# Gathering expert rows in two rounded passes, with the router worked by token tile and expert places released earlier

## The reference

```python
g_prob = softmax((xt @ w_rg) + b_rg)                  # 4 groups
g_w, g_idx = top_k(g_prob, 1)
e_logits = ((xt @ w_re) + b_re).reshape(t, 4, 8)      # 8 experts in each group
e_top, e_loc = top_k(e_logits of the chosen group, 2)
e_w = softmax(e_top) * g_w
# each token goes through its two experts:
y = (silu(xb @ w_gate[e]) * (xb @ w_up[e])) @ w_down[e]
out = sum over both of e_w * y
x = x + gate2 * out ; x = rms_norm(x, g_final)
```

## Time and profile before

| | us |
|---|---|
| runs shown | 1332.38, 1331.24, 1333.41 (median 1332.38) |
| the profiled execution | 1332.06 |
| span of the profile (first to last instruction) | 1329.5 |
| TensorE busy | 1306.5 (98%) |
| VectorE busy | 792.0 (60%) |
| ScalarE busy | 566.5 (43%) |
| mean transfer rate | 280 GB/s |

### The profile page before, as it was taken

How to read it: one execution, slowest core, us unless ns; L and a number is a source line. 1 busy time by engine, 2 the same in 40 slices (tenths; PEclk the granted TensorE clock), 3 DMA queues, 4 the chain that set the end, 5 groups by cost and what they waited for, 6 DMA issues and landing times.

```text
span 1329.5 us, 19339 instructions
## 1 busy us (share of the span) xinstructions
PE 1306.5 (98%) x7854; PEld 969.7 (73%) x7854; DVE 792.0 (60%) x1397; ACT 566.5 (43%) x859; POOL 33.7 (3%) x55
## 2 busy tenths in 40 slices
PE   8999999999999999999999999999999999999997
PEld 8988789999887997999987888754444544444442
DVE  5755598888986655898896877743222322223223
ACT  5344545655546576655645746531111111111122
POOL 0200010000001000100010000000000000000000
PEclk9999999999999999999999999999999999999999
DMA  9467286767585732555665563599999999999995
GB/s 355 162 223 260 100 303 226 237 210 252 202 289 174 241 140 96 183 188 178 252 226 190 209 250 127 197 400 409 428 428 426 429 429 427 429 427 427 428 422 206
DMA packets 113373, 371.83 MB, mean 280 GB/s; under 512 B 4604, under 2 KB 64284, under 8 KB 100368
## 3 DMA queue, kind: packets, MB, share of 16 engines
q1 hardware_dynamic: 105648, 344.07, 67.2%
q0 software_dynamic: 7648, 26.72, 5.7%
HBM read 369.71 MB, written 1.05 MB: 279 GB/s over the span
## 4 chain that ended last, share of the span: by engine, by line
PE 86%; DMA 7%; DVE 4%; ACT 2%; SPq 1%; issue 1%; DVEq 0%; ACTq 0%
PE ps L675 15%; PE ps L1590 14%; PE ps L635 9%; PE ps L636 9%; PE ps L637 9%; PE ps L1613 7%; PE ps L1572 4%; PE ps L652 4%; PE ps L654 3%; PE ps L653 3%; DMA arena<-in_w_expert_gate_dram 3%; DMA arena<-in_w_expert_down_dram 3%; PE ps L1619 2%; DVE w_low L570 1%; DMA const<-in_const_dram 1%; PE ps L1264 1%
## 5 line engine op out<-in xcount | busy, mean ns | idle before, releaser
L570 DVE TENSOR_TENSOR w_low<-ring,w_high 128x1024 fp32r<-128x1024 f32 x264 | 311.4, 1221 | 96.9 <-ACT w_high L562 96.1
L562 ACT ACTIVATE w_high<-ring 128x1024 fp32r<-128x1024 f32 x264 | 264.6, 1050 | 177.0 <-PE ps L675 82.9
L635 PE MATMUL ps<-h_high,w_high 128*128 128x256 f32 x1088 | 310.5, 285 | 0.8 <-DVE h_low L479 0.6
L636 PE MATMUL ps<-h_low,w_high 128*128 128x256 f32 x1088 | 307.8, 283 | 0.0
L637 PE MATMUL ps<-h_high,w_low 128*128 128x256 f32 x1088 | 307.7, 283 | 0.0
L635 PEld LDWEIGHTS ps<-h_high,w_high 128*128 128x128 f32 x1088 | 208.6, 192 | 6.4 <-issue 4.4
L636 PEld LDWEIGHTS ps<-h_low,w_high 128*128 128x128 f32 x1088 | 208.7, 192 | 0.0
L637 PEld LDWEIGHTS ps<-h_high,w_low 128*128 128x128 f32 x1088 | 208.6, 192 | 0.0
L1590 PE MATMUL ps<-ring,arena 128*64 128x512 f32 x592 | 176.6, 594 | 3.0 <-DMA arena<-in_w_expert_gate_dram 1.3
L1590 PEld LDWEIGHTS ps<-ring,arena 128*64 128x64 f32 x592 | 56.3, 137 | 111.8 <-issue 111.7
L675 PE MATMUL ps<-w_high,h_high 128*128 128x512 f32 x304 | 95.0, 394 | 1.0 <-DVE arena L2379 0.9
(11 more groups left out here) (402 smaller groups left out, 1679.8 us busy)
## 6 DMA issues: line engine op xcount, KB each, us to landing
ring<-in_ffn_w_up_dram SPq DMA_DIRECT2D x44, 1024.0 KB, 7.7
ring<-in_w_expert_gate_dram SPq DMA_DIRECT2D x19, 2048.0 KB, 25.0
ring<-in_w_expert_up_dram SPq DMA_DIRECT2D x18, 2048.0 KB, 21.5
ring<-in_w_expert_down_dram SPq DMA_DIRECT2D x17, 2048.0 KB, 26.2
ring<-in_ret_w_in_dram SPq DMA_DIRECT2D x11, 2048.0 KB, 8.0
arena<-in_w_expert_up_dram SPq DMA_DIRECT2D x11, 2048.0 KB, 27.7
ring<-in_ffn_w_down_dram SPq DMA_DIRECT2D x10, 2048.0 KB, 8.3
arena<-in_w_expert_gate_dram SPq DMA_DIRECT2D x9, 2048.0 KB, 23.1
```

Source lines behind the costliest of these rows:

```text
L562: nc.scalar.activation(hi, raw, ACT.Copy).then_inc(hi_done, 1)
L570: last = eng.tensor_tensor(lo, raw, hi.bitcast(F32), ALU.subtract)
L635: nc.tensor.matmul(o, hi, hTh[:, k, :], start=(k == 0 if whole else n == 0), stop=False, skip_group_check=not whole)
L636: nc.tensor.matmul(o, hi, hTl[:, k, :], start=False, stop=False, skip_group_check=not whole)
```

## The change

- `gather` becomes two rounded passes. ScalarE writes the normed rows rounded (`xn_hi`, in the place of `xn`), VectorE writes what is left (`rows_low`: x times the root, less the high part) into `xn_lo`. The low part of tile 1 lies over `rowv` and that of tile 0 over a stretch before it; `sel` becomes fp32r. Per feature block and token tile there are now two matmuls, high and low, each with a stationary tile of its own: 32 rounded matmuls in a gather in place of 16 four-byte ones.
- The first gather (pair 0) is written out by token tile: high of tile 0, high of tile 1, then low of both.
- The router is worked tile by tile on VectorE: `logits`, `group`, `experts`, `position`, `first_select` for tile 0, then for tile 1. Squares and roots go by tile. Casts of the indices fall away (the comparison is made with the integer index); iota counts from 1.
- `idle_turns` in the router go. The starting sums of tile 1 and the matmuls for the largest count move into the middle of gate of pair 0 (`start_second`).
- Places: home 6 waits for `l_t` 2 and not for `b_oc` 4, which takes an attention buffer (`mb_pT`) out of its way; the order of homes changes; half of the tile in home 1 is loaded after the third split of mix_out; one of the homes 4 and 5 (`EARLIER`) is loaded one half of mix_out earlier. Home 9 now comes after the first quarters of `first_downs`.
- The last norm's row `g_last` is loaded during gate of pair 0 over constants that are no longer read, and no longer into `rowv`.

```diff
-        HOMES = (8, 7, 2, 0, 1, 6, 3, 4, 5, 9)
+        EARLIER, LATER = 4 + n_halves % 2, 5 - n_halves % 2
+        HOMES = (8, 7, 2, 6, 0, 1, EARLIER, 3, LATER, 9)
...
+                if home == 1:
+                    sp.wait_ge(lo_done, halves["mix_out"] + 3)
+                    sp.dma_start(dst[:, 0:2, :], src[:, 0:2, :]).then_inc(piece_in, 16)
+                    sp.wait_ge(*freed[holder[home]])
+                    sp.dma_start(dst[:, 2:4, :], src[:, 2:4, :]).then_inc(done, 16)
+                    continue
                 if home < 3:
                     sp.wait_ge(*freed[holder[home]])
+                elif home == EARLIER:
+                    sp.wait_ge(wide_mm, n_halves - 1)
                 elif home == 9:
-                    sp.wait_ge(t_lg, 3)
-                    sp.wait_ge(norm_sd, ROUTED + 1 + NT)
+                    first_quarters()
+                    sp.wait_ge(t_lg, 6)
+                    sp.wait_ge(norm_lo, KD * (N_TR[5] + 1) + NT)
+                    sp.wait_ge(norm_sd, ROUTED + 2 * NT)
                 elif home < 6:
                     sp.wait_ge(wide_mm, n_halves)
                 else:
-                    sp.wait_ge(b_oc, 4)
+                    sp.wait_ge(l_t, 2)
...
+            pool.wait_ge(t_lg, 7)
+            pool.dma_start(g_last, A["g_final_2"].rearrange("(a d) -> a d", a=1).broadcast_to([P, D]))\
...
+            def first_rows(t, low, half):
+                for k in range(4 * half, 4 * half + 4):
+                    part = xn_lo[t][:, k * P:(k + 1) * P] if low else xn_hi[:, t, k * P:(k + 1) * P]
+                    last = nc.tensor.matmul(ps[:, 4 + half, (k % 4) * P:(k % 4 + 1) * P], part, sel[:, t, :],
...
             for t in range(NT):
                 routed_turn(pe, t)
...
+                routed_logits(t)
+
+            start_sum(0, 0)
+            pe.wait_ge(t_rank, 1)
+            nc.tensor.matmul(ps[:, 5, 0:NE], before_m, asg[:, 0, :], start=True, stop=True).then_inc(t_lg, 1)
+            start_sum(0, 1)
+            pe.wait_ge(m_s, 1)
+            pe.wait_ge(norm_sd, ROUTED + 3)
+            for half in range(2):
+                first_rows(0, False, half)
...
+            def start_second():
+                start_sum(1, 0)
+                start_sum(1, 1).then_inc(t_lg, 1)
...
             def gather(j, half, i=None):
...
                 for k in range(4 * half, 4 * half + 4):
                     for t in range(NT):
-                        last = nc.tensor.matmul(ps[:, 4 + half, (k % 4) * P:(k % 4 + 1) * P],
-                                                xn[:, t, k * P:(k + 1) * P], sel[:, t, :],
-                                                start=(t == 0), stop=(t == NT - 1))
+                        for low in range(2):
+                            part = xn_lo[t][:, k * P:(k + 1) * P] if low else xn_hi[:, t, k * P:(k + 1) * P]
+                            last = nc.tensor.matmul(ps[:, 4 + half, (k % 4) * P:(k % 4 + 1) * P], part, sel[:, t, :],
+                                                    start=(t == 0 and not low), stop=(t == NT - 1 and low == 1))
...
+            routed_mean(0)
+            routed_root(0)
+            routed_evict_t1_low(dve)
+            logits(0)
+            group(0)
+            routed_mean(1)
+            experts(0)
+            routed_root(1)
+            logits(1)
+            position(0)
+            first_select(0)
+            group(1)
+            experts(1)
+            rows_low(0)
+            position(1)
+            first_select(1)
+            rows_low(1)
```

More of the change, by code:

```diff
@@ L1535, in _, with routed_logits @@
             project(pe, "mix_out", last_heads, last_outs)
+            def routed_logits(t):
+                for k in range(KD):
+                    if t == 0 and k % 4 == 0:
+                        pe.wait_ge(norm_ha, 2 + k // 4 + 1)
+                    if t == 1 and k in (0, 2):
+                        pe.wait_ge(norm_hv, 2 + k // 2 + 1)
+                    if t == 1 and k == 4:
+                        pe.wait_ge(norm_ha, 2 + 3)
+                    last = nc.tensor.matmul(ps[:, 7 if t else 4, 0:NR], hT[:, k, t * P:(t + 1) * P], wrs[:, k, :],
+                                            start=(k == 0), stop=(k == KD - 1))
+                last.then_inc(t_lg, 1)
@@ new lines, in start_sum @@
+            def start_sum(t, half):
+                return nc.tensor.matmul(ps[:, 2 * t + half, :], ident, x[:, t, half * C:(half + 1) * C], start=True,
+                                        stop=False, skip_group_check=True)
+            def first_rows(t, low, half):
+                for k in range(4 * half, 4 * half + 4):
+                    part = xn_lo[t][:, k * P:(k + 1) * P] if low else xn_hi[:, t, k * P:(k + 1) * P]
+                    last = nc.tensor.matmul(ps[:, 4 + half, (k % 4) * P:(k % 4 + 1) * P], part, sel[:, t, :],
+                                            start=(t == 0 and not low and k % 4 == 0), stop=(t == NT - 1 and low),
+                                            skip_group_check=True)
+                return last
@@ L1538, in _ @@
             for t in range(NT):
                 routed_turn(pe, t)
[L1540 to L1543, removed]
-                                            wrs[:, k, :], start=(k == 0), stop=(k == KD - 1))
-            last.then_inc(t_lg, 1)
+                routed_logits(t)
+            start_sum(0, 0)
@@ L1547, in _ @@
+            pe.wait_ge(m_s, 2)
+            pe.wait_ge(norm_sd, ROUTED + 4)
+            for half in range(2):
+                first_rows(1, False, half)
             for t in range(NT):
+                pe.wait_ge(norm_lo, KD * (N_TR[5] + 1) + t + 1)
                 for half in range(2):
-                    nc.tensor.matmul(ps[:, 2 * t + half, :], ident, x[:, t, half * C:(half + 1) * C], start=True,
-                                     stop=False, skip_group_check=True)
-            idle_turns(4, 6, T)
@@ L1558, in _ @@
-            idle_turns(2, 6, T)
-            pe.wait_ge(norm_sd, ROUTED + 1 + NT)
+                    part = first_rows(t, True, half)
+                    if t:
+                        part.then_inc(m_ga, 1)
+            def start_second():
+                start_sum(1, 0)
+                start_sum(1, 1).then_inc(t_lg, 1)
+                nc.tensor.matmul(ps[:, 7, 128:128 + NE], ones, asg[:, 0, :], start=True, stop=False)
+                nc.tensor.matmul(ps[:, 7, 128:128 + NE], ones, asg[:, 1, :], start=False, stop=True).then_inc(t_lg, 1)
@@ L1580, in enter_tile, with gate_or_up @@
                 return HOMES[N % NS]
[L1582 removed]
+            def gate_or_up(j, g, i=None, middle=None):
                 if g == 0:
@@ L1586, in gate_or_up @@
                 for k in range(KD):
+                    if k == KD // 2 and middle is not None:
+                        middle()
                     if g == 0 and k == KD // 2:
@@ L1704, in expert_pass @@
                     pe.wait_ge(m_y, 2 * first)
-                for half in range(2):
-                    gather(first, half)
-                gate_or_up(first, 0)
+                    for half in range(2):
+                        gather(first, half)
+                gate_or_up(first, 0, None, None if r else start_second)
                 turn_select(first)
```

271 lines of the change are left out of this document (142 added, 129 removed).

## The result

The changed kernel takes 1336.1 us (median of seven executions, 1334.9 to 1338.3), the kernel before 1331.5 beside it: a ratio of 1.0035, 95% interval 1.0025 to 1.0046. One of the seven executions of the kernel before took 2282.57 us, the other six 1330.4 to 1333.4. The changed kernel is slower by 4.6 us, 2.5 more than the 1333.6 that was forecast and inside the range. The profiled execution took 1335.67 us, its span is 1333.7, 4.2 more than in the earlier trace rows.

What follows compares the result with a forecast made beforehand. Weight transfers after the first down's end were taken to bound the kernel. Router 1.2 us earlier, sums 2.3 and gather 0.1 later put the end 1.2 later: span 1330.7, plus 2.56 and 0.32, 1333.6; range 1329.0 to 1337.5.

Steps and rivals of the forecast that it cites:

- the term that was costed at nothing: Router: the `idle_turns` taken out were said to have only filled gaps, so no time was counted for them.
- a dearer pass: Rival, gathers: pass at 0.125 us, 0.44 us more a pair, 1335.2 by TensorE's limit; chance 0.19 together with lower clock.
- a lower clock: Rival, first gate: TensorE's gaps in the router lower its clock, up to 4 us; chance 0.19 together with dearer pass.
- End and first down: Expert stage: queue full from the first down's end on, so the end follows it by 403 us; both 1.2 later.
- Whatever was loaded sooner: Expert stage: the end moves with the first down's end, regardless of earlier loads; places freed sooner counted at nothing.
- Its tile is wanted a pair later: SP's queue: home 9, now behind the quarter loads, holds a tile needed a pair later; counted at nothing.
- The norm row's 1.2 us: Gate of pair 0: loading the final norm's row, 0.5 MB, falls where the queue isn't full: 0, at most 1.2.
- The gather: Every pair: 32 rounded passes at 0.111 to 0.120 us plus 0.21 fixed; 3.91 us, 0.14 more a pair.
- quick loads: Rival, gathers: rounded weight loads are quicker, passes 0.067 us apart, first gather 1.42 us shorter: 1332.1; chance 0.17.
- The router: Router worked by tile: gate of pair 0 starts at 877.7, 1.2 us earlier, with 1.0 to either side.
- The sums in the gate: Gate of pair 0: tile 1's starting sums and rank matmuls move in, 2.3 us on the path.
- that go only filled gaps: Router: the `idle_turns` taken out were said to have filled gaps only, with no time counted for their removal.

Runs made afterwards that it cites:

- e5_places_back: The changed kernel with the old order and waits of the homes other than home 9: 1336.02 us (1.0033).
- e3_no_idle: The kernel before without the router's six `idle_turns`, nothing else: 1333.28 us (1.0012).
- e4_four_byte: The changed kernel with the gather in four-byte form again and no low rows: 1330.42 us (0.9993).
- e10_home9: e2_sums with home 9 loaded once the last start sum is done, ahead of the quarters: 1331.33 us (1.0004).
- e12_all: The changed kernel with four-byte gather, no low rows, start sums early, home 9 ahead of quarters, ScalarE's copies ahead of its exponentials, `g_last` late: 1328.81 us (0.9981).
- e6_early: The kernel before with four more 512-column passes, results unused, in the middle of the first gate: 1335.18 us (1.0030).
- e7_late: The kernel before with four more 512-column passes, results unused, in pair 11 between up and gather: 1331.56 us (1.0000).
- e11_glast_late: The changed kernel with `g_last` loaded by SyncE behind the last expert tile: 1336.22 us (1.0031).
- e2_sums: The changed kernel with tile 1's start sums moved from the first gate to behind the ranks: 1334.66 us (1.0020).
- e1_fill: The changed kernel with `idle_turns` put back into the router, one ahead of tile 1's ranks, four ahead of its selection: 1335.49 us (1.0027).
- e9_high_only: The changed kernel with the gathers of pairs 1 to 15 cut to their high parts, 16 passes for 32: 1336.47 us (1.0033).
- e13_rounded_all: As e12_all, but with the gather in two rounded passes with its low rows: 1330.08 us (0.9992).

## Why the prediction came out as it did

The time lay in the range, the sign of the shift was right, and the size was off by the term that was costed at nothing. The range was wide enough to take in the rival that came true: 1336.1 lies just above the forecast's own bounds (1332.4 to 1336.0), in the band that the prediction gave to a dearer pass or a lower clock (1335 to 1340). In span the miss is 3.0 us (4.2 more than before, where 1.2 was forecast). That the time missed by only 2.5 is luck: the profiled execution of the kernel before had 2.56 us around its span, that of the changed kernel 1.97.

- **End and first down.** Right for this kernel (403.4 against 403.3 us), but by luck, since the second limit lay within about 1 us of the first; incomplete as a rule. "Whatever was loaded sooner" is true of the early places (e5_places_back), but what is loaded *later* counts. "Its tile is wanted a pair later" looked at when TensorE needs home 9, and not at the queue that must move it ahead of tiles 12 to 15. The norm row's 1.2 us, put at 0, lies in that queue too. The rule with two events, against the spans of the profiled executions:

| kernel | tiles 14, 15 issued | queue through (estimate) | later + 424.8 | span |
|---|---|---|---|---|
| before | 904.72 | no pause | 1329.5 | 1329.5 |
| changed | 908.81 | 909.3 | 1334.1 | 1333.7 |
| e3_no_idle | 907.49 | no pause | 1332.3 | 1331.8 |
| e4_four_byte | 902.73 | 903.1 | 1327.9 | 1327.7 |
| e10_home9 | 904.71 | 902.4 | 1329.5 | 1329.5 |
| e12_all | 901.80 | 898.3 | 1326.6 | 1326.5 |
| e6_early | 908.41 | no pause | 1333.2 | 1332.8 |
| e5_places_back | 909.30 | 908.9 | 1334.1 | 1334.2 |
| e7_late | 905.70 | no pause | 1330.5 | 1330.8 |
| e11_glast_late | 909.47 | 907.6 | 1334.3 | 1335.1 |
| e2_sums | 904.15 | 906.3 | 1331.1 | 1332.8 |
| e1_fill | 907.43 | 907.9 | 1332.7 | 1333.9 |
| e9_high_only | 906.92 | 908.2 | 1333.0 | 1334.5 |
| e13_rounded_all | 906.75 | 900.5 | 1331.6 | 1332.8 |

The constant 424.8 is the row of before. "Queue through" is the first issue after the pause, plus 0.9, plus 25.8 (24.6 where `g_last` is late). Where home 9 goes first (e10_home9, e12_all, e13_rounded_all) the queue runs low again ahead of the quarters, so the estimate is too early; the release is the later event there all the same. The last four lie 1.2 to 1.7 above. In all four the last up takes 8.78 us in place of 7.09, with a mean granted clock of 0.83 to 0.90 from 1290 to 1300: that is the lower clock behind a late wait. The 0.8 of e11_glast_late stay open.

- **The gather.** Right in its price of a pass, at the lower bound. A gather takes 1.94 + 1.74 = 3.68 us and not 3.91, 0.09 less than the lowest that was stated: 32 x 0.111 and 0.13 fixed in place of 0.21. The rounded loads last 192 ns as those in the earlier trace rows:

```profile
L1640 PEld LDWEIGHTS ps<-last_selection_turned,xn_low 128*128 128x128 f32 x240 | 46.0, 192 | 0.0
L1640 PEld LDWEIGHTS ps<-last_selection_turned,xn_high 128*128 128x128 f32 x240 | 46.0, 192 | 12.2 <-issue 12.2
```

e9_high_only shows that fewer passes in the later gathers gain nothing. The rivals with quick loads and with a dearer pass both fall. The Trainium skill ("TensorE: Matmul & The Clock Gate", Weight-path perf modes) excludes FP32 from its fast load; by these rows the rounded type loads no faster.

- **The router.** The gate would start at 877.65, as e2_sums shows at full clock; forecast 877.7. That this agrees so well is in part luck: the low rows cost 2.05 and 2.12 us, near the upper price (2.2), 0.7 more for both than the middle that was taken, and other steps of its chain were shorter by about as much:

```profile
870.42 2.05 DVE L2782 SCALAR_TENSOR_TENSOR xn_low<-x_hT,stat,xn_high 128x1024 fp32r<-128x1024 f32 x1
...
872.81 2.12 DVE L2782 SCALAR_TENSOR_TENSOR xn_low<-x_hT,stat,xn_high 128x1024 fp32r<-128x1024 f32 x1
```

- **The sums in the gate.** Right: 2.3 us on the path, as forecast.
- **The `idle_turns`.** This is the step that failed: "that go only filled gaps". The clock's loss is 879.07 - 877.65 = 1.4 us ahead of the gate and 5.18 - 3.58 = 1.6 in it, 3.0 of the 4.1 us. That the missing `idle_turns` let the clock fall is shown by e3_no_idle, for the kernel before. The prediction had it as a rival ("up to 4 us") and set it low because the clock stood at 1.00 in every stretch read. But those stretches had the `idle_turns` in them: they showed the clock with its cover, not without. The tally of the first down is then -1.2 (router) + 2.3 (sums) + 3.0 (clock) = 4.1, where the prediction had -1.2 + 2.3 + 0.1.

Whether the clock alone, held at 1.00 with the sums left in the gate, would give the forecast's 1333.6 is not shown: e1_fill held it only to 876.

## What to carry to other kernels

Work with unused results beside a wait may be what keeps TensorE's clock up: before it is taken out, read the clock with the gap open, not with it filled. In a stream that is full to the end, ask of each load that moves later what the queue still has to move before its next release, and not only when the tile is used. And where two limits lie within a microsecond, mending one shows nothing: e2_sums and e11_glast_late each looked like a small or no gain, the two edits of e10_home9 together gave all 4.8 us back.

## What the hardware showed

- The granted clock fell to 0.50 (1.2 GHz) at 872, in TensorE's wait of 1.76 us for the second selection, stayed there although the gather's passes went on, and returned within the first gate, at 882. The low passes of the first gather take 3.62 us for 16, 0.226 each, twice 0.111. The Trainium skill ("TensorE: Matmul & The Clock Gate", Part 1: The HAM clock gate) has half the clock as the idle state; in this trace short waits between matmuls were enough for it.
- The same fall comes late in the kernel behind a wait of about 2 us for weights, and not always: behind 2.18 (e2_sums) and 1.84 us (e1_fill) it came, behind 2.38 (e3_no_idle) and 1.78 us (changed) not. The time goes with it from execution to execution: of the ten of e10_home9 six took 1330.0 to 1331.5 us at a mean clock of 0.998, four 1333.0 to 1334.0 at 0.995 or 0.996. Where the clock fell in those four no trace shows; in the profiled execution of e13_rounded_all (mean clock 0.994) it fell twice, in the first gate and behind the last up's wait of 2.42 us.
- A VectorE pass over 128x1024 that reads one operand turned took 2.05 to 2.12 us against the 1.23 of the plain addition. The operation itself is little dearer: unturned it took 0.75 us for 512 columns (L2247 of the kernel before), where an addition took 0.69 (L2174).
